# Gate and up products of a feed-forward block: one 512-column matmul for both parts of x, halves added on VectorE, four PSUM banks instead of two

## The reference

```python
def swiglu(x, w_gate, w_up, w_down):
    return (jax.nn.silu(x @ w_gate) * (x @ w_up)) @ w_down

def first_block(x, ...):
    for layer in range(DEPTH):                                   # 2 layers
        x = x + 0.5 * swiglu(rms_norm(x, norm_ffn1[layer]), ...)  # feed-forward 0, 2
        ...                                                       # attention and its projections
        x = x + 0.5 * swiglu(rms_norm(x, norm_ffn2[layer]), ...)  # feed-forward 1, 3
    return x
```

## Time and profile before

| what | us |
|---|---|
| median of three runs | 2277.57 |
| the three runs | 2272.53, 2277.57, 2286.49 |
| span of the profiled execution | 2282.9 |
| TensorE busy in it | 2021.8 |
| VectorE busy in it | 1273.8 |
| ScalarE busy in it | 805.0 |

### The profile page before, as it was taken

How to read it: one execution, slowest core, us unless ns; L and a number is a source line. 1 busy time by engine, 2 the same in 40 slices (tenths; PEclk the granted TensorE clock), 3 DMA queues, 4 the chain that set the end, 5 groups by cost and what they waited for, 6 DMA issues and landing times.

```text
span 2282.9 us, 35219 instructions
## 1 busy us (share of the span) xinstructions
PE 2021.8 (89%) x14096; PEld 1635.6 (72%) x14096; DVE 1273.8 (56%) x2331; ACT 805.0 (35%) x1336; POOL 651.1 (29%) x671
## 2 busy tenths in 40 slices
PE   7999989999999999999988999986887677668867
PEld 7999979999999979999777988872333322224425
DVE  5555636555654664654565443385666566656543
ACT  5444335444443554443663322221211222112212
POOL 0000010000000100000002322047777777777772
PEclk9999999999999999999999998998899989999989
DMA  9653507554564514563305001579999999999994
GB/s 309 193 180 125 185 1 229 195 184 148 185 193 142 180 57 142 196 197 127 117 1 177 29 21 39 171 266 378 371 382 353 373 373 359 356 374 375 374 375 149
DMA packets 254878, 489.60 MB, mean 214 GB/s; under 512 B 13936, under 2 KB 174224, under 8 KB 254624
## 3 DMA queue, kind: packets, MB, share of 16 engines
q0 software_dynamic: 73888, 268.53, 31.3%
q1 hardware_dynamic: 177104, 214.32, 28.8%
q10 hardware_dynamic: 3760, 5.02, 0.7%
HBM read 486.74 MB, written 1.05 MB: 214 GB/s over the span
## 4 chain that ended last, share of the span: by engine, by line
PE 67%; POOL 14%; issue 6%; DMA 5%; DVE 5%; ACT 3%; POOLq 0%; DVEq 0%; ACTq 0%
PE bank L778 67%; POOL arena_sb L2792 11%; POOL con_sb L2792 3%; DMA arena_sb<-peer_u,arena_sb 2%; DMA con_sb<-peer_v,arena_sb 1%; DMA arena_sb<-peer_v,arena_sb 1%; DVE parts_sb L2103 0%; PE bank L969 0%; DVE xT_sb L2167 0%; DVE parts_sb L2098 0%; DVE sq_sb L2664 0%; DMA xT_sb<-xT 0%; ACT parts_sb L1623 0%; DMA ring_sb<-w_in 0%; DMA ring_sb<-ffn_w_gate 0%
## 5 line engine op out<-in xcount | busy, mean ns | idle before, releaser
L778 PE MATMUL bank<-arena_sb 64*64 64x64 f32 (+7 forms) x3688 | 514.2, 323 | 154.3 <-ACT arena_sb L2054 117.4
L778 PE MATMUL bank<-xh_sb,parts_sb 128*128 128x256 f32 x3328 | 605.1, 284 | 19.7 <-DVE parts_sb L2098 16.3
L778 PEld LDWEIGHTS bank<-arena_sb 64*64 64x64 f32 (+4 forms) x3688 | 299.7, 161 | 360.6 <-issue 216.6
L778 PEld LDWEIGHTS bank<-xh_sb,parts_sb 128*128 128x128 f32 x3328 | 514.9, 190 | 26.0 <-issue 25.0
L778 PE MATMUL bank<-xl_sb,parts_sb 128*128 128x256 f32 x1808 | 510.2, 282 | 0.0
L2664 DVE CUSTOM_DVE_ANT_0 sq_sb<-arena_sb 128x1024 f32<-128x1024 f32 x256 | 309.7, 1224 | 263.9 <-DMA arena_sb<-peer_u,arena_sb 263.2
L2098 DVE TENSOR_TENSOR parts_sb<-ring_sb,parts_sb 128x2048 fp32r<-128x2048 f32 x132 | 298.7, 2290 | 173.1 <-ACT parts_sb L1609 173.1
L778 PEld LDWEIGHTS bank<-xl_sb,parts_sb 128*128 128x128 f32 x1808 | 343.9, 190 | 0.0
L2792 POOL DMA_INDIRECT arena_sb<-peer_u,arena_sb x256 | 284.3, 1111 | 191.6 <-DVE arena_sb L2612 107.7
L1609 ACT ACTIVATE parts_sb<-ring_sb 128x2048 fp32r<-128x2048 f32 x132 | 248.1, 1910 | 69.8 <-PE bank L778 68.5
L778 PE MATMUL bank<-h_high_sb,parts_sb 128*128 128x256 f32 x1408 | 255.9, 283 | 0.0
(11 more groups left out here) (274 smaller groups left out, 1865.7 us busy)
## 6 DMA issues: line engine op xcount, KB each, us to landing
ring_sb<-ffn_w_gate SPq DMA_DIRECT2D x44, 1024.0 KB, 5.4
ring_sb<-ffn_w_up SPq DMA_DIRECT2D x44, 1024.0 KB, 6.6
ring_sb<-ffn_w_down SPq DMA_DIRECT2D x44, 1024.0 KB, 4.9
ring_sb<-w_in SPq DMA_DIRECT2D x17, 1024.0 KB, 6.0
ring_sb<-w_in_ab SPq DMA_DIRECT2D x12, 1024.0 KB, 5.3
ring_sb<-w_out SPq DMA_DIRECT2D x12, 1024.0 KB, 5.3
ring_sb<-w_in_cd SPq DMA_DIRECT2D x12, 1024.0 KB, 5.4
ring_sb<-peer_w_q SPq DMA_DIRECT2D x8, 1024.0 KB, 5.3
```

The lines of the kernel that those rows point to most:

```text
L778: return pe.matmul(dst, lhsT, rhs, start=start, stop=stop_, skip_group_check=loose)
```

## The change

`xh` and `xl` become the two halves of one tile, `xhl`, at the same addresses. For gate and up, `mm_wide` replaces `mm3`: the high part of the weight meets both parts of x in one matmul of 512 columns, and the low part of the weight meets x high in one of 256 columns. So a bank's left half holds high by high plus low by high, its right half high by low, and gate and up need a bank each: 4 and 5 for even chunks, 6 and 7 for odd ones. VectorE adds the halves of each bank by a `tensor_reduce` over the pair (two of them, 512 elements in, 256 out), waits for its own result (`summed`), and only then multiplies by `rstd`. TensorE waits for `summed` in place of `scaled` before it writes the banks again. Since bank 7 also holds the sum of squares, up of chunk 1 waits until that has been read. `down` and all the projections keep `mm3`.

```diff
-        xh = fast("xh", [P, KC, T], xn_at)
-        xl = fast("xl", [P, KC, T], sq_at)
+        xhl = fast("x_high_low", [P, 2, KC, T], xn_at)
+        xh, xl = xhl[:, 0, :, :], xhl[:, 1, :, :]
...
+            def mm_wide(b, fixed_hi, fixed_lo, moved, start, stop_):
+
+                first = mm(b[:, 0 : 2 * T].rearrange("p (a t) -> p a t", a=2), fixed_hi, moved, start, False, True)
+                return first, mm(b[:, 0:T], fixed_lo, moved[:, 0, :], False, stop_, True)
...
-                    b, s, g = bank[4 + c % 2], c % 2, c // 2
+                    s, g = c % 2, c // 2
                     if c >= 2:
-                        pe.wait_ge(scaled, base + c - 1 + 4 * i)
+                        pe.wait_ge(S("summed"), base + c - 1 + 4 * i)
                     for j, kind in enumerate(("gate", "up")):
+                        b = bank[4 + 2 * (c % 2) + j]
+                        if c == 1 and j == 1:
+                            emptied(pe, ("ssq", n))
...
-                            first, ins = mm3(b[:, j * T : (j + 1) * T], hi[:, kk, cols], lo[:, kk, cols],
-                                             xh[:, kk, :], xl[:, kk, :], kk == 0, kk == KC - 1)
+                            first, ins = mm_wide(b, hi[:, kk, cols], lo[:, kk, cols], xhl[:, :, kk, :], kk == 0, kk == KC - 1)
...
-                    dve.tensor_tensor(GU[c % 2][:, :, :], bank[4 + c % 2][:, :].rearrange("p (a b) -> p a b", a=2),
+                    for j in range(2):
+                        b = bank[4 + 2 * (c % 2) + j]
+                        ins = dve.tensor_reduce(GU[c % 2][:, j, :], b[:, 0 : 2 * T].rearrange("p (a t) -> p t a", a=2), AX.X, ALU.add)
+                    ins.then_inc(S("summed"), 1)
+                    dve.wait_ge(S("summed"), base + c + 1 + 4 * i)
+                    dve.tensor_tensor(GU[c % 2][:, :, :], GU[c % 2][:, :, :],
                                       rstd[:, :].unsqueeze(1).broadcast_to([P, 2, T]), ALU.mult).then_inc(scaled, 1)
```

More of the change, by code:

```diff
@@ L212, in build @@
         xh_ready, hraw_ready, hh_ready = sem("xh_ready"), sem("hraw_ready"), sem("hh_ready")
-        xh = fast("xh", [P, KC, T], xn_at)
-        xl = fast("xl", [P, KC, T], sq_at)
+        assert sq_at == xn_at + 4 * KC * T
+        xhl = fast("x_high_low", [P, 2, KC, T], xn_at)
+        xh, xl = xhl[:, 0, :, :], xhl[:, 1, :, :]
         PAIR = {("gate", 0): 8192, ("up", 0): 12288, ("gate", 1): 0, ("up", 1): 4096, ("down", 0): 16384, ("down", 1): 16384}
```

## The result

| what | before | after |
|---|---|---|
| median, us | 2273.32 (6 runs, 2269.93 to 2286.49) | 2306.73 (6 runs, 2295.98 to 2309.13) |
| ratio, 95% interval | | 1.0119 (1.0097 to 1.0141) |
| profiled execution, span | 2282.9 | 2294.2 (timed at 2295.98) |

By the ratio the changed kernel is 1.2% slower, about 27 us (22 to 32); the two medians lie 33 us apart. The forecast was 2294 us, 0.7% slower; the range 2266 to 2316 holds the time.

The account below looks back on a forecast made before the run. TensorE was taken to bound the steady loop, its saving waited away behind VectorE and ScalarE. Edges of 3.9 us a block, +15.6 in four, plus 1 for the clock, put +17 on 2277.6: 2294 us, range 2266 to 2316.

Parts of the forecast that it names:

- What bounds: Steady feed-forward loop: TensorE sets 17.07 us a group of two chunks, hiding VectorE and ScalarE's 14.41 with 2.66 to spare.
- TensorE's share: Gate and up matmuls: new pair 333 ns in place of 355.3, 32 us less of TensorE's time, group 16.35 us.
- D: Delay of each chunk's silu, product, high and low parts after VectorE has begun, from the reductions: 1.33 us.
- VectorE's share: Reductions in each chunk: VectorE busier by 121 us, its group with ScalarE 17.07 us, so TensorE's saving is waited away.
- The edges: First and last chunks of each block no longer cancel: 3.9 us a block, +15.6 us in four blocks.
- the bare end: Last chunk of each block: the reductions' 1.33 us stands uncovered, counted as +1.3 us a block.
- The clock: TensorE at half clock after its idle time at down(2): at most 0.5 us a block, 2 in all; 1 added.
- the long wait: TensorE idle before down(2), the down product of chunk 2, until the weight split comes: 4.5 us.
- TensorE stays the bound: Rival for the steady loop: TensorE's saving shows if D is under 0.97; 2261 us, or 2249; chance 0.10.
- The stride: Rival for VectorE's reductions: reading PSUM elements 1 KB apart makes D 2.39, 85 us more, 2379 us; chance 0.12.
- A longer chain: Rival for VectorE's new wait in the hardware loop: it costs more, D 1.50, 14 us more, 2308 us; chance 0.12.

Follow-up runs that it names:

- pe_shorter: The changed kernel without three of the sixteen low-by-high matmuls of each chunk, part of gate and up missing; 2302.58 us, ratio 1.0110.
- patterns: The changed kernel with test matmuls ahead of its first block: wide-and-short pairs, triples, matmuls sorted by length, pairs into separate banks; 2392.55 us, one run.
- rates: The changed kernel with some 370 test matmuls ahead of its first block, in runs of one kind each; 2393.34 us, one run.

## Why the prediction was right, and where it was not

**What bounds.** The reading that TensorE sets the loop, with VectorE and ScalarE hidden under it by 2.66 us a group, was right: taking 1.33 us twice used it up. The number that carried it, 14.41 us for the hidden loop out of the first chunks of a block, gave 17.07; pe_shorter, in which that loop alone sets the pace, reads 17.04.

**TensorE's share: the mis-sized term.** The pair was to take 333 ns, "an `fp32r` matmul of 512 columns; I take half of" the float32 one. It takes 353, outside the bounds of 323 to 343.5 that I gave. The saving is 2 ns a pair, 3 us in all, not 22.5 and 32. The upper bound assumed the 11.8 ns to stick to any matmul; a matmul of 512 costs 13.5 alone, and in the kernel 8 more (235 ns to the next start), of which patterns lays 5 to the change of length. The row that the 214.4 came from was read as a whole float32 matmul, and it is one of the two records that such a matmul leaves (48 for the 24 in rates); half of a record is still one run of 512 columns, so this didn't change the number. Trainium skill, "TensorE: Matmul & The Clock Gate", section LDWEIGHTS, gives a weight load of P columns P / 1.2 ns, an estimate of 107 for 128: the floor of 110 that rates shows agrees with it. By the same estimate a load is shorter than the 213 ns of 512 columns in front of it, so this rule doesn't explain the 13.5 ns.

That error cost little, because the forecast already had the saving waited away. That it cost little is luck: with D well under 0.97 the 32 us would have stood in the forecast, and it would have missed by most of them. But it wasn't free. I had TensorE at 16.35 and VectorE at 17.07, one loop clearly the longer. In truth both are 17.05 to 17.1, and they hand work to each other both ways: VectorE waits for TensorE once in a group (0.34 us above), TensorE for the low split in every second one (0.25, 0.16), and a group takes 17.31 on average. pe_shorter shows that the 0.25 goes when TensorE's loop is shorter; that two equal loops can't both be kept fed is my reading of it. Nine groups make 2.1 us a block.

**VectorE's share.** D was sized right: 1.32 measured for 1.33. The steps 9.63 and 7.42 were forecast as 9.63 and 7.44. VectorE is busy for 110 us more and not 121: two reductions take 1.28 us together, not 1.38, since the second starts before the first ends.

**The edges**, by the fourth block, which has no half clock: 180.4 - 175.7 = 4.7 us for the 21 steps where 3.1 - 0.4 = 2.7 was forecast. Of the 2.0 between them, the nine groups are +2.1, the last step +0.35 (no shorter gate_up), the one before it +0.1, and the step from chunk 0 to 1 is -0.56: 7.43 instead of 7.99. A row that I hadn't used explains this last one. ScalarE loads its table for the silu behind `rstd`, before and after:

```profile
565.12 1.28 ACT L1662 ACT_TABLE_LOAD   x1
566.42 0.42 ACT L1667 ACTIVATE sgate_sb<-sgate_sb 128x256 f32<-128x256 f32 x1
```

```profile
580.09 1.28 ACT L1670 ACT_TABLE_LOAD   x1
582.16 0.42 ACT L1675 ACTIVATE sgate_sb<-sgate_sb 128x256 f32<-128x256 f32 x1 [0.78 <-DVE sgate_sb L2156]
```

Before, the silu of chunk 0 waited for the table, not for VectorE: it began 566.42 - 565.14 = 1.28 after the multiply. Now the reductions run beside the load, and it begins 2.05 after the first of them. Only 0.77 of D shows in that step. The start of the blocks and the bare end cost 2.7 by the fourth block where (1.3 x 3 - 0.2 x 4) = 3.1 was forecast, closer than the stages between the blocks repeat.

**The clock.** Half clock behind the long wait was forecast at 1 us, 2 at most. The wait was shorter than forecast (2.9 us for 4.5, since chunk 1 is 0.56 earlier and TensorE later), yet it brought the half clock in three blocks of four and 5.7 us. The reasoning that failed was "a step where 1.0 is spare": that spare was the saving of the pair, which isn't there. 3.4 us at half clock are 1.7 us of TensorE's work, and blocks 2 and 3 are longer than the fourth by 1.5, so almost nothing is absorbed. In pe_shorter, where TensorE does have the spare time, 6.8 us at half, 3.4 of work, lengthen the two steps behind the wait by only about 2. It also reached further than one stretch of 3.3 us: in the first block it lasted 6.8.

In sum: 4 x 4.7 + 5.7 + 2.7 + 1.3 for the last end = 28.5, where the prediction had 15.6 + 1. The time measured is 27 (22 to 32).

**The rivals.** *TensorE stays the bound* would have needed D under 0.97; it is 1.32. *The stride* is refuted: the reductions of pairs that lie 1 KB apart in PSUM take 0.68 to 0.69 us (88 + 88 of them, median 681 and 682 ns), no longer than 512 elements in a row take. Groups of the line by form, ns minimum, median, maximum:

```profile
L2153 DVE TENSOR_REDUCE sgate_sb<-bank x88: 673/681/692, 29.3 to 1100.4; 128x256 f32<-128x512 f32 x88
L2153 DVE TENSOR_REDUCE hT_sb<-bank x88: 678/682/694, 36.7 to 1108.9; 128x256 f32<-128x512 f32 x88
```

The Trainium skill, Advanced Engine Details and Errata, section Memory Cachelines, says of PSUM that every two consecutive elements should be contiguous, and of SBUF that a different line per access costs; it names matmuls as what suffers in PSUM. For VectorE reading PSUM these 176 reductions don't bear it out. *A longer chain* is refuted by the same 1.32. So the time lay above the forecast's own range of 2284 to 2304 through two steps, the pair's saving that isn't there (with the longer groups and last step that follow) and the half clock, not through a rival.

## What to carry to other kernels

Before making one engine's instructions cheaper, find how long the loop of the *other* engines is when it runs alone, with its waits in it: the first steps after a late start show it, and a busy share of 56% doesn't. When work is added to the hidden loop, see which instruction in its queues is late for no reason; moving one copy ahead of a silu gave back 15 of 27 us here. And a rate for an instruction of another format or length is a guess, however near it looks: its bounds must hold a saving of nothing.

## What was not expected of the hardware

- An `fp32r` matmul of 512 columns takes 227 ns, 13.5 more than its columns at 2.4 GHz, alone and without DMA beside it; one of 256 takes 120, one of 128 takes 110; a float32 one of 512 leaves two records of 429, each 2 more than twice its columns.
- Long and short matmuls in turn take 353 ns a pair; sorted by length they take 348 in a test ahead of the blocks, and 352 in the kernel.
- A pause of 2.9 us in TensorE was followed, 1.3 us after its end, by 3.4 us at half clock, and 24 matmuls in the pause prevented it, in all four blocks. Of ten pauses of 2.8 to 3.0 us at this place seven had half clock behind them, of ten of 0.7 to 1.5 us none.
- VectorE sums pairs of floats 1 KB apart in PSUM as fast (681 ns for 512) as it reduces 512 in a row (688).
